# One output tile of a 2048-wide projection computed in two parts: 96 columns as three fp32r products, 32 columns as one fp32 product

## The reference, cut to what matters

```
o = jnp.concatenate([o_a, o_b], axis=-1).astype(h.dtype)
out = jnp.einsum('bte,ed->btd', o, p['w_out_even'][j])
...
x = x + rms_norm(mix, p['norm_mix_post'][l])
```

## Time and profile before

| | us |
|---|---|
| three runs | 3572.92, 3574.46, 3575.01 (median 3574.46) |
| the profiled execution | 3568.65 |
| its span | 3566.6 |
| stage `out_even` in it | about 907 to 1025 from the span's start |
| TensorE matmul busy | 3352.9 (94%) |
| VectorE (DVE) busy | 1917.7 (54%) |
| ScalarE (ACT) busy | 1253.8 (35%) |

### The profile page before, as it was taken

One profiled execution on the slowest core, in us unless ns is written; L12 is line 12 of the kernel. 1 busy time (PEld: TensorE's weight loads), 2 busy tenths in 40 slices (PEclk: granted clock), 3 DMA queues, 4 the chain that ended last, 5 costly groups with the idle time before them and its releaser, 6 DMA issues.

```text
span 3566.6 us, 61189 instructions
## 1 busy us (share of the span) xinstructions
PE 3352.9 (94%) x24672; PEld 3239.9 (91%) x24672; DVE 1917.7 (54%) x2317; ACT 1253.8 (35%) x1582; POOL 460.1 (13%) x400
## 2 busy tenths in 40 slices
PE   8998896858899999999999999998999999999997
PEld 8998885847889999999999899986989999999997
DVE  5446667584566454355544666924475543455444
ACT  5344343232353332233333435321453332233332
POOL 0018774000000000000000035920000000000000
PEclk9999997979899999999999999986999999999999
DMA  6443331000444454454444544533444444445543
GB/s 200 150 143 108 120 108 56 3 26 16 147 131 148 147 150 155 138 151 147 149 159 142 194 147 120 172 137 136 147 130 148 147 154 153 135 147 152 157 146 110
DMA packets 118662, 474.88 MB, mean 133 GB/s; under 512 B 13425, under 2 KB 15089, under 8 KB 115569
## 3 DMA queue, kind: packets, MB, share of 16 engines
q1 hardware_dynamic: 108864, 421.58, 38.4%
q10 hardware_dynamic: 9648, 51.17, 3.7%
HBM read 450.66 MB, written 22.03 MB: 133 GB/s over the span
## 4 chain that ended last, share of the span: by engine, by line
PE 88%; DVE 7%; ACT 2%; issue 1%; POOL 1%; DMA 0%; ACTq 0%; DVEq 0%; POOLq 0%
PE ps L348 49%; PE ps L352 25%; PE ps L1842 1%; PE ps L312 1%; PE ps L317 1%; PE ps L322 1%; PE ps L1862 1%; PE ps L1416 1%; PE ps L957 1%; PE ps L1418 1%; PE ps L1380 0%; PE ps L1365 0%; PE ps L935 0%; PE ps L1597 0%; DVE hEa L886 0%
## 5 line engine op out<-in xcount | busy, mean ns | idle before, releaser
L348 PE MATMUL ps<-x_hi,w_hi 128*128 128x320 f32 x4768 | 1424.1, 312 | 39.9 <-DVE x_lo L548 28.7
L288 ACT ACTIVATE w_hi<-raw 128x1024 fp32r<-128x1024 f32 (+1 forms) x756 | 842.0, 1114 | 1741.3 <-PE ps L352 1688.4
L348 PE MATMUL ps<-x_lo,w_hi 128*128 128x320 f32 x4768 | 1415.6, 310 | 0.0
L296 DVE TENSOR_TENSOR w_lo<-raw,w_hi 128x1024 fp32r<-128x1024 f32 (+1 forms) x640 | 834.5, 1306 | 788.3 <-ACT w_hi L288 775.7
L348 PEld LDWEIGHTS ps<-x_hi,w_hi 128*128 128x128 f32 x4768 | 902.1, 189 | 48.3 <-issue 30.7
L348 PEld LDWEIGHTS ps<-x_lo,w_hi 128*128 128x128 f32 x4768 | 902.1, 189 | 0.9
L352 PE MATMUL ps<-x_hi,w_lo 128*128 128x320 f32 x4768 | 800.9, 310 | 11.4 <-POOL w_lo L296 11.2
L352 PEld LDWEIGHTS ps<-x_hi,w_lo 128*128 128x128 f32 x4768 | 726.1, 189 | 15.2 <-POOL w_lo L296 14.3
L296 POOL TENSOR_TENSOR w_lo<-raw,w_hi 128x1024 fp32r<-128x1024 f32 x116 | 302.8, 2616 | 1682.2 <-ACT w_hi L288 1680.4
L348 PE MATMUL ps<-u_hi,w_hi 128*128 128x320 f32 x1408 | 416.6, 310 | 8.3 <-DVE u_lo L610 8.3
L348 PE MATMUL ps<-u_lo,w_hi 128*128 128x320 f32 x1408 | 416.1, 310 | 0.0
(11 more groups left out here) (374 smaller groups left out, 2902.9 us busy)
## 6 DMA issues: line engine op xcount, KB each, us to landing
raw<-in_w_ffn_in SPq DMA_DIRECT2D x352, 512.0 KB, 3.6
raw<-in_w_ffn_out SPq DMA_DIRECT2D x128, 704.0 KB, 4.1
raw<-in_w_in_even SPq DMA_DIRECT2D x116, 512.0 KB, 3.6
raw<-in_w_in_odd SPq DMA_DIRECT2D x96, 512.0 KB, 3.6
raw<-in_w_out_even SPq DMA_DIRECT2D x32, 512.0 KB, 3.6
raw<-in_w_out_odd SPq DMA_DIRECT2D x32, 512.0 KB, 3.6
hS<-in_state_hgrn ACTq DMA_DIRECT2D x4, 1024.0 KB, 4.9
out_hgrn_s<-hS ACTq DMA_DIRECT2D x4, 1024.0 KB, 5.1
```

The costliest lines, as they stand in the source:

```text
L288: nc.scalar.activation(w_hi[s % 2][:, 0:g.kt, :], raw[s % 4][:, 0:g.kt, :], ACT.Copy)\
L296: eng.tensor_tensor(w_lo[s % 2][:, 0:g.kt, :], raw[s % 4][:, 0:g.kt, :], w_hi[s % 2][:, 0:g.kt, :].bitcast(f32), sub).then_inc(sem(f"split ...
L348: nc.tensor.matmul(out, w_hi[s % 2][:, k, :], x[:, kk, :], start=half == 0 and k == 0 and x is xh, stop=False)
```

## The change

Units n = 6 and n = 7 of `out_even`, that is its output tile 3, are no longer multiplied by `multiply_unit` but by a new function. It forms features 0 to 95 of the tile from the split operands as before, with 96 weight columns instead of 128, and features 96 to 127 from the unsplit fp32 weights in `raw` and the unsplit mixer output in `Z`. The `raw` buffer is now read by PE until the end of the unit, so SP waits for `unit_done` before it loads units n = 10 and n = 11 over it.

```diff
@@ ring_load
                 if s >= 4:
                     split_wait(sp, i, s - 4)
+                if g is plan["out_even"] and s - 4 - g.unit0 in NARROW:
+                    sp.wait_ge(sem("unit_done"), s - 3)
@@ new
+        NARROW = (6, 7)
+
+        def narrow_unit(pe, s, xh, xl):
+
+            g = owner[s]
+            half, tile = s % 2, g.tile0 + (s - g.unit0) // 2
+            pe.wait_ge(sem("split_hi"), s + 1)
+            if half == 0:
+                pe.wait_ge(sem("tile_out"), tile - 3)
+            out = PS[tile % 4][:, 0:T]
+            for k in range(g.kt):
+                kk = half * g.kt + k
+                for x in (xh, xl):
+                    nc.tensor.matmul(out[0:96], w_hi[s % 2][:, k, 0:96], x[:, kk, :],
+                                     start=half == 0 and k == 0 and x is xh, stop=False)
+            split_wait(pe, 0, s)
+            for k in range(g.kt):
+                nc.tensor.matmul(out[0:96], w_lo[s % 2][:, k, 0:96], xh[:, half * g.kt + k, :], start=False,
+                                 stop=half == 1 and k == g.kt - 1)
+            raw_wait(pe, 0, s)
+            for k in range(g.kt):
+                kk = half * g.kt + k
+                mm = nc.tensor.matmul(out[96:128], raw[s % 4][:, k, 96:128], mixer_part(kk // 2)[:, kk % 2, :],
+                                      start=half == 0 and k == 0, stop=half == 1 and k == g.kt - 1)
+            mm.then_inc(sem("unit_done"), 1)
@@ multiply_unit
+            if g is plan["out_even"] and n in NARROW:
+                narrow_unit(pe, s, xh, xl)
+                return
```

## The result

The changed kernel took 3595.19 us (median of 3 runs, 3594.47 to 3606.01) against 3574.46 us before: 20.7 us more, ratio 1.0068, 95% interval 1.0039 to 1.0098. Forecast were 9.4 us more and a range up to 3590.5 us. The direction was right, the size was not: it is more than double. The profiled execution took 3595.19 us with a span of 3593.3 us, 26.7 us longer than the span before.

A forecast was written before the change was run, and what follows sets the result against it. PE, busy without a gap, was taken to bound the changed stage. fp32r 0, fp32 blocks 8.60, tile changes 0.80 and waits 0 made 9.4 us, from 3574.46 to 3583.9 us; the 8 in 10 range was 3580 to 3590.5 us.

The forecast's parts named there:

- What bounds the stage: In out_even PE is busy without a gap, so a microsecond more on PE is one more at the end.
- fp32r at 96 columns costs nothing and saves nothing: The 48 fp32r matmuls of units n = 6 and 7 stay at 147 ns each: 0 us difference.
- The bounds of -0.6 and +2.0 us: Limits for the 48 fp32r matmuls: 0.6 us gained at pure streaming time, 2.0 us lost if weight loads set the pace.
- A block is 4.30 us: Eight fp32 matmuls per changed unit, 538 ns each, take 4.30 us; two blocks 8.60 us.
- A change of tile costs 0.20 us: PE changes array tile into and out of each fp32 block, four times at 0.20 us: 0.80 us.
- Waits and loads cost nothing: PE's wait for raw_full, the later unit_done and SP's added waits around the changed units: 0, at most 1.3 us.
- The clock at the blocks: Rival, 12%: the fp32 blocks bring PE's clock to 0.50, 5.8 us more for both, 3589.7 us.
- The sum: Whole kernel: 0 + 8.60 + 0.80 + 0 = 9.4 us on PE, all on the path, giving 3583.9 us.

The follow-up runs named there:

- c1_noblock: The changed kernel without its 16 fp32 matmuls, so features 96 to 127 of tile 3 are not computed: 3571.34 us, ratio 0.9998 to the kernel before.
- c2_wide: The changed kernel with its fp32 matmuls 128 weight columns wide, into a bank nobody reads, without a change of array tile: 3599.99 us.
- c2_pad47: The kernel before with 47 further dense fp32r matmuls behind the full-width units n = 6 and 7, 6.9 us more PE work: 3578.97 us.

## Why the prediction was wrong

Point by point:

- *What bounds the stage*: right. 9.2 us more on PE in the two units are 9.2 us more at the end of the stage (35.0 to 44.2 us in the table).
- *fp32r at 96 columns costs nothing and saves nothing*: right, 3.52 us for a unit in c1_noblock. The bounds of -0.6 and +2.0 us were not needed.
- *A block is 4.30 us*: right to the digit; c2_wide shows 7.82 us for unit and block. So at 320 columns moved an fp32 matmul with 32 weight columns takes as long as one with 128.
- *A change of tile costs 0.20 us*: 0.15 us, 0.6 us in all instead of 0.8. The Trainium skill, "TensorEngine Tiling (Array Packing)", section Key Properties, says that changing the tiling mode drains TensorE; the trace agrees that there is a price, and c2_wide gives its size.
- *Waits and loads cost nothing*: right. Behind the blocks the units are again 3.52 us apart, and c1_noblock with the same waits is as fast as before.
- *The clock at the blocks*: the rival did not occur; it was 1.00 over both. Narrow tiles with 320 columns moved did not bring it down in the 4.3 us of a block. That this rival's 3589.7 us lies nearer to the measured time than the forecast is luck: what was lost to the clock was lost elsewhere.
- *The sum*: "0 + 8.60 + 0.80 + 0 = 9.4 us on PE, all of it on the path", and from there the same 9.4 us for the whole. This step failed. It took for granted that all stages behind the change keep their length when they begin 9 us later. The retention stage doesn't: 9.6 or 14.1 us more in its stretch. The even layer's channel mixer doesn't either: 2.0 us more, of which 1.5 us are the fall of the clock behind PE's wait; no experiment was made on it by itself.

The rows that would have raised the question were there. The earlier trace rows were read for the price of a lower clock at the blocks, and found their way into the rival at 12%. They show a stage in which the granted clock goes down and up again while PE's records leave no pause. That stage lasts 115 us in the kernel before, and as the runs showed its length depends on when it starts; the question "what happens there if it starts 9 us later" was not asked. The rows of before alone could not have given the size. The shifts measured do: from 8.6 to 10.3 us of shift the cost was 7.0 to 26.1 us, and of the ten rows of the table five lie within 3.2 us of the shift alone and five lie 11 to 18 us above it, with nothing between.

In the retention stage PE's records cover 115.2 of 115.2 us (c2_pad47), and the clock falls on matmuls that move 8 columns per weight load. The Trainium skill, "TensorE: Matmul & The Clock Gate", section "HAM oscillation — how this bites in real kernels", puts the clock's fall down to idle gaps of PE between bursts of matmuls. In the retention stage the trace shows no such gap. There is one of 0.82 us ahead of its first dense matmul, in both kernels, but in the kernel before the clock falls again 31.7, 59.0 and 86.3 us behind the first thin matmul, and PE's records leave no gap in between. But the ends of matmuls in a trace are modelled, and how much of a thin matmul the array spends at work cannot be read from them, so this does not refute the rule. In the channel mixer the fall does stand behind a gap, the wait of 2.07 us; yet the kernel before has the same gap and no fall.

## What to carry to other kernels

A kernel with a stage in which the granted clock alternates may have no fixed length behind a change: here a shift of 1.8 us cost 16.3 us, and one of 10.2 us cost 7.0 us. Look for such stages in the row of the clock before summing; time a change to the stages ahead also with a small pad of dense matmuls behind it, and read the effect in its own stretch, not in the total. With 320 columns moved, narrowing the weight columns from 128 to 96 (fp32r) or to 32 (fp32) saved no time.

## What the runs showed of the hardware

- The clock fell in a stretch in which PE's records leave no gap. A head's thin stretches of 16 matmuls (32 records) take 3.74 us at full clock and 6.99 us at half.
- The same wait of PE, 2.07 us, was followed by 3.4 us at half the clock in the changed kernel and by none in the kernel before.
- The retention stage took discrete values over many shifts, in its stretch 385.5, 395.1, 399.6 or 399.7, and 402.3 us. The two executions of the kernel before agreed to 0.1 us although they had reached out_even 8 us apart; those of the changed kernel differed by 4.6 us. What aligns an execution with the clock's changes ahead of that stage was not tried.
- An fp32 matmul with 320 columns moved takes 538 ns at full clock, whether it has 32 or 128 weight columns. Its weight load does get shorter in the rows, to no effect:

```profile
L350 PEld LDWEIGHTS ps<-Z,raw x32: 106/110/110, 943.0 to 955.0; 128*32 128x32 f32 x32
L350 PE MATMUL ps<-Z,raw x32: 432/432/457, 943.1 to 955.2; 128*32 128x320 f32 x32
```
